# Norm sums in four strips of 65 tokens, their reciprocals spread by the identity's columns, in a decoder step on one core

## What is computed

```python
def _rms(x, g):
    y = x32 * lax.rsqrt(jnp.mean(x32 * x32, axis=-1, keepdims=True) + RMS_EPS)
    return y * g

h = h + 0.5 * post1(SwiGLU_1(pre1(h)))
u = pre_m(h);  [qA kA vA qB kB vB gA gB] = u @ w_in
h = h + post_m(((sigmoid(gA) * (oA @ p_a)) + (sigmoid(gB) * (oB @ p_b))) @ w_o)
h = h + 0.5 * post2(SwiGLU_2(pre2(h)))
```

## Time and profile before

| | |
|---|---|
| Runs | 1292.88, 1292.99 and 1298.64 us, median 1292.99 |
| Profiled execution | 1299.55 us, its span 1297.8 us |
| TensorE busy | 1258.3 us, 97% of the span |
| VectorE busy | 585.6 us, 45% |
| ScalarE busy | 403.5 us, 31% |
| Mean granted TensorE clock | 0.987 |

### The profile page before, as it was taken

The page is one execution under the profiler, slowest core; times in us unless marked ns, Lnnn a source line. Parts: engine busy times, 40 slices in busy tenths (PEclk is TensorE's granted clock), DMA queues, the critical chain, the costliest instruction groups (busy, mean ns, idle before and its releaser), DMA issues.

```text
span 1297.8 us, 24456 instructions
## 1 busy us (share of the span) xinstructions
PE 1258.3 (97%) x10532; PEld 1217.2 (94%) x10532; DVE 585.6 (45%) x886; ACT 403.5 (31%) x660; POOL 5.2 (0%) x31
## 2 busy tenths in 40 slices
PE   6999999999999899999999999998999999999996
PEld 5999999999999899988988899997999999999995
DVE  6343443433337512545567723758543443433335
ACT  6221222212224432344445532435312222112221
POOL 0000000000000000000000000000000000000000
PEclk9999999999999899999999999999999999999998
DMA  5222222222222133302123175122122222222211
GB/s 198 66 97 97 97 80 82 97 89 90 90 90 83 63 110 123 102 34 82 52 96 132 50 250 206 66 98 66 66 97 97 72 90 97 97 89 90 90 58 67
DMA packets 30218, 123.14 MB, mean 95 GB/s; under 512 B 4442, under 2 KB 12658, under 8 KB 18418
## 3 DMA queue, kind: packets, MB, share of 16 engines
q1 hardware_dynamic: 30146, 122.09, 27.5%
HBM read 115.39 MB, written 6.67 MB: 94 GB/s over the span
## 4 chain that ended last, share of the span: by engine, by line
PE 92%; DVE 4%; ACT 2%; issue 1%; DVEq 1%; DMA 1%; SPq 0%; ACTq 0%
PE bank L1204 28%; PE bank L1205 27%; PE bank L1206 27%; PE bank L1229 1%; PE bank L1450 1%; PE bank L1396 1%; PE bank L1385 1%; PE bank L1467 1%; PE bank L1457 1%; PE bank L1358 1%; PE bank L1349 1%; DVE w_lo L869 1%; DVEq L863 1%; DVE f L910 1%; ACT w_hi L527 1%
## 5 line engine op out<-in xcount | busy, mean ns | idle before, releaser
L1204 PE MATMUL bank<-u_hi,w_hi 128*128 128x260 f32 x2144 | 618.1, 288 | 12.5 <-DVE u_lo L898 12.5
L1205 PE MATMUL bank<-u_lo,w_hi 128*128 128x260 f32 x2144 | 608.4, 284 | 0.0
L1206 PE MATMUL bank<-u_hi,w_lo 128*128 128x260 f32 x2144 | 608.2, 284 | 0.0
L1204 PEld LDWEIGHTS bank<-u_hi,w_hi 128*128 128x128 f32 x2144 | 406.9, 190 | 30.9 <-issue 28.3
L1206 PEld LDWEIGHTS bank<-u_hi,w_lo 128*128 128x128 f32 x2144 | 407.0, 190 | 0.0
L1205 PEld LDWEIGHTS bank<-u_lo,w_hi 128*128 128x128 f32 x2144 | 406.8, 190 | 0.1
L527 ACT ACTIVATE w_hi<-raw 128x2048 fp32r<-128x2048 f32 x87 | 166.2, 1910 | 314.6 <-PE bank L1206 314.5
L869 DVE TENSOR_TENSOR w_lo<-raw,w_hi 128x2048 fp32r<-128x2048 f32 x51 | 116.9, 2291 | 223.1 <-ACT w_hi L527 205.2
L1204 PE MATMUL bank<-hid_hi,w_hi 128*128 128x260 f32 x704 | 199.4, 283 | 0.0
L1205 PE MATMUL bank<-hid_lo,w_hi 128*128 128x260 f32 x704 | 199.0, 283 | 0.0
L1206 PE MATMUL bank<-hid_hi,w_lo 128*128 128x260 f32 x704 | 198.8, 282 | 0.0
(11 more groups left out here) (183 smaller groups left out, 1038.5 us busy)
## 6 DMA issues: line engine op xcount, KB each, us to landing
raw<-w_stream SPq DMA_DIRECT2D x90, 1024.0 KB, 4.9
raw<-w_stream SPq DMA_DIRECT2D x8, 768.0 KB, 4.4
h<-x_t SPq DMA_DIRECT2D x8, 260.0 KB, 5.6
y_t<-h SPq DMA_DIRECT2D x8, 260.0 KB, 2.6
slot_a<-vb_pool SPq DMA_DIRECT2D x8, 256.0 KB, 4.5
ka_t<-k_a SPq DMA_DIRECT2D x2, 520.0 KB, 3.0
kb_t<-k_b SPq DMA_DIRECT2D x2, 520.0 KB, 3.0
va_o<-v_a SPq DMA_DIRECT2D x2, 512.0 KB, 5.0
```

The source lines that it names most:

```text
L1204: pe.matmul(out_of(b), w, hi_x, start=first, stop=False)
L1205: pe.matmul(out_of(b), w, lo_x, start=False, stop=False)
L1206: return pe.matmul(out_of(b), v, hi_x, start=False, stop=last)
```

## The change

The ones matrix is cut to 32 columns, and a sum goes to four strips: partitions 32s to 32s+31 of the bank hold the sums of tokens 65s to 65s+64, in columns 0 to 64. Each f32 product of 260 columns so becomes four of 65 columns with 32 output partitions. Root and reciprocal then work on 65 columns instead of 260. `widen` brings the reciprocals back to all partitions: for each strip one f32 product of 65 columns whose stationary operand is column 32s of the identity repeated 128 times, into columns 128 to 387 of the same bank. VectorE's scalings read them there. Both go through two new semaphores: TensorE waits for `rinv_made` ahead of a widening, VectorE for `rinv_wide` behind its reciprocal. VectorE's drains around the reciprocal go.

Where a widening stands in TensorE's list: behind the sum (start, group 0; last norm); behind chunk 0's second tile (start, group 1); behind the output tile in which the post norm's sum stands (`sum_post` group 0); ahead of `keep_clock` (pre norm, group 0); behind chunk n's second tile (post norm, group 1); behind the sum (pre norm, group 1). The sum `sum_h(q, 1)` moves from the middle of the third tile to behind the fourth. At the start the identity's load moves ahead of the first weights on SP's queue, VectorE takes the first norm ahead of chunk 0's low part and the second ahead of chunk 1's, and ScalarE makes `u_hi` of group 1 ahead of chunk 1's high part.

```diff
@@ -34,6 +34,7 @@
 T = SEQ + DEC
 G = 2
 TG = T // G
+QS = TG // 4
 FF = 2816
 CW = 256
 CH = KD * CW
@@ -273,6 +276,15 @@
         def out_of(b):
             return bank[b][:, 0:TG]
 
+        def strip_of(s):
+
+            return slice(32 * s, 32 * s + 32), slice(s * QS, (s + 1) * QS)
+
+        def wide_of(sums, g, n=1):
+
+            x = sums[g][:, P:P + TG].rearrange("p (a c) -> p a c", a=1)
+            return x if n == 1 else x.to_broadcast([P, n, TG])
+
         def fold_view(src, n):
 
             return src[:].rearrange("p (t r j c) -> p t r j c", t=n, r=4 // n, c=32)
@@ -367,11 +379,11 @@
                     part = (slice(None), slice(2 * s, 2 * s + 2), tg(g))
                     sp.dma_start(h[part], x_t[part]).then_inc(x_in[4 * g + s], 16)
                 if g == 0:
+                    sp.dma_start(ident[:], consts[:, 0:P]).then_inc(ident_in, 16)
                     load(0, 0)
                     sp.dma_start(gain[:], gains_in).then_inc(const_in, 16)
                     sp.dma_start(bias_b[:], b_rows).then_inc(const_in, 16)
                     sp.dma_start(pg[0:1, :], pages).then_inc(const_in, 16)
-                    sp.dma_start(ident[:], consts[:, 0:P]).then_inc(ident_in, 16)
             load(1, 1)
             ffn_loads(FFN1)
 
@@ -561,7 +573,7 @@
             def take_root(src, summed, count, g):
 
                 act.wait_ge(summed, count)
-                act.activation(root[:, g, :], src[g][:, 0:TG], ACT.Sqrt, bias=eps[:, 0:1],
+                act.activation(root[:, g, 0:QS], src[g][:, 0:QS], ACT.Sqrt, bias=eps[:, 0:1],
                                scale=1.0 / D).then_inc(root_made, 1)
 
             def u_top(q, g):
@@ -671,8 +683,8 @@
             act.wait_ge(consts_ready, 3)
             u_top(0, 0)
             take_root(sum_pre, h_summed, 16, 1)
+            u_top(0, 1)
             hi(1)
-            u_top(0, 1)
             for b in range(4):
                 silu_out(b, R_FFN1 + 1)
             ffn_up(FFN1, R_FFN1)
@@ -879,16 +891,18 @@
                 dve.tensor_tensor(w_lo[:, a, half:CH], raw[:, a, half:CH], w_hi[:, a, half:CH].bitcast(F32),
                                   ALU.subtract).then_inc(lo_made, 1)
 
+            def inverse(roots, g):
+
+                dve.wait_ge(root_made, roots)
+                dve.reciprocal(rinv[:, g, 0:QS], root[:, g, 0:QS]).then_inc(rinv_made, 1)
+                dve.wait_ge(rinv_wide, roots)
+
             def u_scale(q, g):
 
-                dve.wait_ge(root_made, pre_root(q, g))
-                drain()
-                dve.reciprocal(rinv[:, g, :], root[:, g, :])
-                drain()
+                inverse(pre_root(q, g), g)
                 for s in range(4):
                     part = (slice(None), slice(2 * s, 2 * s + 2), tg(g))
-                    dve.tensor_tensor(f[part], h[part], rinv[:, g:g + 1, :].to_broadcast([P, 2, TG]),
-                                      ALU.mult).then_inc(hn_made, 1)
+                    dve.tensor_tensor(f[part], h[part], wide_of(sum_pre, g, 2), ALU.mult).then_inc(hn_made, 1)
                 drain()
 
             def u_low(q, g, tiles=range(KD)):
@@ -901,13 +915,10 @@
 
             def h_of(p, g, between=None):
 
-                dve.wait_ge(root_made, post_root(p, g))
-                drain()
-                dve.reciprocal(rinv[:, g, :], root[:, g, :])
-                drain()
+                inverse(post_root(p, g), g)
                 for s in range(4):
                     part = f[:, 2 * s:2 * s + 2, tg(g)]
-                    dve.tensor_tensor(part, part, rinv[:, g:g + 1, :].to_broadcast([P, 2, TG]), ALU.mult)
+                    dve.tensor_tensor(part, part, wide_of(sum_post, g, 2), ALU.mult)
                 if between is not None:
                     between()
                 drain()
@@ -989,12 +1000,12 @@
             dve.wait_ge(const_in, 48)
             for site in (1, 5):
                 dve.tensor_scalar(gain[:, site, :], gain[:, site, :], 0.5, None, ALU.mult).then_inc(consts_ready, 1)
+            u_scale(0, 0)
             lo_by_halves(0, 1)
-            u_scale(0, 0)
             u_low(0, 0)
-            lo(1)
             u_scale(0, 1)
             u_low(0, 1)
+            lo(1)
             ffn_up(FFN1, R_FFN1)
             outputs(0, FFN1 + 2 * UPS)
 
@@ -1226,12 +1237,27 @@
             def sum_h(q, g):
                 for t in range(KD):
                     pe.wait_ge(h_sq, 16 * q + 8 * g + t + 1)
-                    pe.matmul(sum_pre[g][:, 0:TG], ones[:], sqh[t % 4], start=t == 0,
-                              stop=t == KD - 1).then_inc(h_summed, 1)
+                    for s in range(4):
+                        rows, cols = strip_of(s)
+                        mm = pe.matmul(sum_pre[g][rows, 0:QS], ones[:, 0:32], sqh[t % 4][:, cols], start=t == 0,
+                                       stop=t == KD - 1)
+                    mm.then_inc(h_summed, 1)
 
             def sum_out(p, g):
                 pe.wait_ge(acc_added, out_at(p, DNS - 1, 2 * g + 1) + 1)
-                pe.matmul(sum_post[g][:, 0:TG], ones[:], acc[:, g, :], start=True, stop=True).then_inc(post_summed, 1)
+                for s in range(4):
+                    rows, cols = strip_of(s)
+                    mm = pe.matmul(sum_post[g][rows, 0:QS], ones[:, 0:32], acc[:, g, cols], start=True, stop=True)
+                mm.then_inc(post_summed, 1)
+
+            def widen(sums, g, roots):
+
+                pe.wait_ge(rinv_made, roots)
+                for s in range(4):
+                    one_row = ident[:, 32 * s:32 * s + 1].to_broadcast([P, P])
+                    mm = pe.matmul(sums[g][:, P + s * QS:P + (s + 1) * QS], one_row, rinv[:, g, 0:QS], start=True,
+                                   stop=True)
+                mm.then_inc(rinv_wide, 1)
 
             def keep_clock(n):
 
@@ -1241,13 +1267,17 @@
             def first_chunks(q, n, r):
 
 
+                widen(sum_pre, 0, pre_root(q, 0))
                 keep_clock(7)
                 pe.wait_ge(lo_made, n + 1)
                 u_item(n % 2, 0, r, q, midway=lambda: sum_out(q - 1, 1))
                 u_item(n % 2, 1, r, q)
+                widen(sum_post, 1, post_root(q - 1, 1))
                 pe.wait_ge(lo_made, n + 2)
-                u_item((n + 1) % 2, 0, r + 1, midway=lambda: sum_h(q, 1))
+                u_item((n + 1) % 2, 0, r + 1)
                 u_item((n + 1) % 2, 1, r + 1)
+                sum_h(q, 1)
+                widen(sum_pre, 1, pre_root(q, 1))
                 for c in range(2):
                     for b in (2, 3):
                         u_item((n + c) % 2, b, r + c, None if c else q)
@@ -1260,6 +1290,8 @@
                         pe.wait_ge(lo_made, n0 + c + 1)
                         for b in range(4):
                             u_item(c, b, r0 + c, None if c else q)
+                            if (c, b) == (0, 1):
+                                widen(sum_pre, 1, pre_root(0, 1))
                 with pe.Fori(1, UPS) as i:
                     for s in range(2):
                         pe.wait_ge(lo_made, n0 + 1 + s + 2 * i)
@@ -1305,6 +1337,7 @@
                     for b in (0, 1):
                         down_item(j % 2, b, r1 + 1, j % KC)
                 down_item(0, 2, r1 + 1, KC - 2, sums=p)
+                widen(sum_post, 0, post_root(p, 0))
                 down_item(0, 3, r1 + 1, KC - 2)
                 down_item(1, 2, r1 + 1, KC - 1)
                 if p < 2:
@@ -1315,6 +1348,8 @@
             for _ in range(5):
                 pe.matmul(sum_post[0][:, 0:P], ones[:], ones[:], start=True, stop=True)
             sum_h(0, 0)
+            pe.wait_ge(ident_in, 16)
+            widen(sum_pre, 0, pre_root(0, 0))
             sum_h(0, 1)
             ffn_up(0, FFN1, R_FFN1)
             ffn_down(0, FFN1 + 2 * UPS, R_FFN1 + 2 * UPS)
@@ -1633,6 +1668,7 @@
                 for b in range(4 if r < DNS - 2 else 2):
                     wo_item(r, b)
             wo_item(DNS - 2, 2, sums=True)
+            widen(sum_post, 0, post_root(1, 0))
             wo_item(DNS - 2, 3)
             wo_item(DNS - 1, 2)
             sum_h(2, 0)
@@ -1640,6 +1676,7 @@
             ffn_up(2, FFN2, R_FFN2)
             ffn_down(2, FFN2 + 2 * UPS, R_FFN2 + 2 * UPS)
             sum_out(2, 1)
+            widen(sum_post, 1, post_root(2, 1))
 
 
 # ---- launch: host layout only
```

More of the change, by code:

```diff
@@ L208, in step_program @@
         root_made = sem("root_made")
+        rinv_made = sem("rinv_made")
+        rinv_wide = sem("rinv_wide")
         hi_half = sem("hi_half")
```

## The result

| | before | after |
|---|---|---|
| median of 20 executions each, measured beside each other, us | 1293.31 (1292.41 to 1299.52) | 1298.78 (1296.88 to 1300.26) |
| profiled execution, us | 1299.55 | 1298.60 |
| its span, us, and mean granted clock | 1297.8, 0.987 | 1296.8, 0.989 |

The account below looks back on a forecast made before the run. TensorE is busy 97% of the span, so gains come only at norms where it waits or runs on its low clock. -0.7 - 0.9 - 1.95 + 0.2 + 0.4 = -3.0 us off the median 1292.99: 1290.0, range 1284.5 to 1295.5.

Parts of the forecast that it names:

- the end: Last norms: the widening of group 0's post norm costs TensorE 0.86 us, the last norm gives 0.64; 0.2 lost.
- Prices: Lengths assumed per operation: reciprocal 0.56 us, root 0.27, sum term 0.22, widening holding TensorE 0.86, tiling change 0.1 each way.
- Cheap widening: Rival: widening records cost only their 65 columns, ten widenings at 0.43 us each, 4.3 us, giving 1285.7; chance 0.24.
- Serial strips: Rival: 32-column loads don't overlap neighbouring strips' products; a term costs 0.65 us, four boundary sums +10.9 us, 1301; chance 0.05.
- I subtract the same from the median: Final step: the 3.0 us saved against the profiled execution of 1299.55 also comes off the median 1292.99, giving 1290.0.
- the term -0.9: Boundary between FFN1 and the input projection: group 1's pre-norm scalings start at 432.85 instead of 433.77, 0.9 us gained.
- the term -1.95: Boundary between the out projection and FFN2: group 1's scalings start at 909.65 instead of 911.62, 1.95 us gained.
- "Clock", +0.4: Boundaries and widenings: one low-clock stretch instead of two, maybe longer, and some widenings at 1.2 GHz; 0.4 us lost.
- The rival "Clock": The merged wait leaves one more low-clock stretch at the start and each boundary: 4.8 us, so 1294.8; chance 0.21.
- The start, -0.7: Start of the kernel: group 1's scalings begin at 25.55 instead of 26.23, behind 48 products and a widening; 0.7 us gained.

Follow-up runs that it names:

- before_again: The kernel before, unchanged, measured and profiled once more: 1294.16 us, ratio 0.9998, profiled execution 1294.01 us.
- fill_start: The changed kernel with filler products at the start alone: 1294.34 us, ratio 0.9993 to the kernel before.
- old_start: The changed kernel with the start of the kernel before (full-width sums, old order), no fillers: 1297.28 us, ratio 1.0018 to the kernel before.

## Why the prediction was wrong, by its own steps

**What it got right.** The chain of operations at each place and most prices. Against the traced execution the first boundary gave 0.9 us as forecast, the second 1.8 (1.95), the end cost nothing (0.2). These agreements hold against that execution alone. The first products of group 1 came at 437.45 and 912.56 (forecast 436.1 and 912.9); the wait that ended at 425.84 is gone, and the merged one stands round a widening.

**Prices.** Reciprocal 0.563 us (0.56), root 0.315 (0.27), last norm 2.50 (2.54). The widening takes 1.00 and holds TensorE from 400.58 to 401.38 and 0.09 in the next product's start, 0.89 (0.86). The scalings read PSUM at 691 ns as before. The change of tiling costs 0.1 us each way: behind the strips one product is listed 0.39 us long and the next starts 0.23 later instead of 0.12, exactly the row. The Trainium skill (TensorEngine Tiling (Array Packing), Key Properties) has the change of mode drain TensorE; the trace shows less than half of one product for it. One price was wrong, and harmlessly: when squares wait, two terms in strips start 0.25 us apart (429.87 and 430.12), 0.125 a term and not 0.22. The squares paced the sums, so it changed nothing.

**Cheap widening** is refuted by the 0.89 us. **Serial strips** is refuted by the 0.125 us a term. The Trainium skill (TensorE: Matmul & The Clock Gate, Part 3) says that a load overlaps running products only where the row groups differ; these eight records with their eight loads share all rows and start every 16 ns, where the 65 columns of one record would hold TensorE for 0.055 us by the earlier trace rows (0.219 for 260). So loads went on while products of other strips ran, and the rule doesn't hold for column strips here.

**The step that failed first: "I subtract the same from the median".** The difference of 3.0 us was made against an execution of 1299.55 and taken off a median of 1292.99, as if a constant lay between them. It wasn't one: against `before_again` that execution had four more low stretches, worth 2.0 us in the sums of the first boundary (5.47 us instead of 3.50), 1.6 in the products behind 437, some 1.5 in those behind 915 and 1.7 near 557. That is 6.8 by the rows, where the two executions differ by 5.5. The first lies inside the term -0.9, the next two right behind the two boundaries. Inside the term -1.95 lies a slow sum too, 903.69, which `before_again` also has. At an even clock in both kernels the two terms are +0.8 and -0.1: both gains were low clock in the kernel before. The prediction had 5.47 and 3.50 in one group and called the first "partly on the low clock" without asking whether the median execution had it; that the sum of group 1 at the second boundary took 5.47 as well it didn't use.

**The term that was mis-sized: "Clock", +0.4.** By the fillers it is 7.6 us in the changed kernel against 3.7 in the kernel before, +3.9. The text held that one low stretch instead of two might come cheaper. Measured, three of the four short waits of `before_again` were passed at full clock, though none in the forecast's execution. The merged wait had the low stretch behind it at both boundaries in all three profiled executions that have it unfilled (after, `fill_start`, `old_start`). The rival "Clock" had the right kind, places and nearly the size, +4.8 for one more low stretch at the start and at each boundary. Its 1294.8 came out too small because the gains to which it was added weren't there.

**The start, -0.7.** It is -0.9 at an even clock and +1.5 as written, each within 1.8. The step took the 48 products at their 5.97 us of before and put the second widening behind them. The change takes 2.4 us of TensorE's work away ahead of them (5.34 to 2.92), and in three of three profiled executions without fillers they then began at 1.2 GHz. The prediction counted the work removed as cost saved and didn't ask what it had been doing for the clock. The forecast also had the widening at 1.0, not 1.94.

**The sum over again**, by what was measured: start -0.9, boundaries +1.1, together +0.2 at an even clock (measured 0.0, within 1.8), and +3.9 of clock: 1293.3 + 4.1 = 1297.4, where the ratio gives 1297.2 and the median is 1298.78. The clock term comes from the same ratios, so this agreement tests only the +0.2.

**What stays open.** Why the clock falls behind the waits of 2.2 and 1.76 us in one execution and not in another of the same program; the low stretch near 557; how far the medians of filled kernels still hold some of it; and what makes executions with the same mean clock differ by up to 4.8 us. That the merged wait is followed by a low clock in every execution isn't shown either: six of six in three traces, and the 7.6 us that the fillers give back on average, speak for it.

## What to carry to other kernels

When a sum of terms is made against one traced execution, first find that execution's place among the others, and list its low-clock stretches with what each costs; a term that only removes one of them isn't a gain on the median. Work of TensorE that looks dispensable ahead of a long run of products, or inside a wait, may be what holds the clock: before it is made smaller, put a filler in its place and time both. And a helper operation of TensorE that another engine waits for belongs inside a tile at the product where its input is ready; that order alone was worth 6.5 to 7.1 us here, and the same change with it and the fillers went from 0.3% slower to 0.6 or 0.7% faster.

## What the runs showed of the hardware that was not expected

- The same waits of TensorE, 2.22 or 2.23 and then 1.76 us, were followed by sums at 1.2 GHz in one execution (5.47 us) and at 2.4 GHz in another (3.50).
- At the head of the trace of the kernel after the granted clock is listed as 1.00 while 15 products in a row come every 0.215 us, the pitch of 1.2 GHz. (In that of `old_start` the column does show the low stretch there.)
- f32 products of 65 columns in four column strips, each with its own load of 32 columns, run at 16 ns a record (16 records in 0.25 us), faster than the packed rows of 128 columns (29 ns).
- 32 filler products at the start and the two boundaries were worth 7.3 us of 1299 in the changed kernel, 27 in the waits of the same places 3.7 to 3.9 in the kernel before.
